# A decoder block with routed experts: another way through the router, and six weight chunks issued from ScalarE

## The reference, cut to what matters

```python
u = rmsnorm(h, norm_mix_w)
p = u @ w_in                       # pool | q,k,v | z | a | b | two branch gates
merged = sigmoid(gA) * pool_branch(p) + sigmoid(gB) * delta_net(p)   # 8 heads of 128
h = h + merged @ w_out
x = rmsnorm(h, norm_ffn_w)
group = argmax(softmax(x @ w_grp + b_grp))           # one of 4 groups
e1, e2 = top2(softmax((x @ w_rtr + b_rtr)[group]))   # two of the group's 8 experts
y = sum over e in (e1, e2) of weight_e * (silu(x @ w_gate[e]) * (x @ w_up[e])) @ w_down[e]
out = rmsnorm(h + y, norm_final_w)[meta:]
```

## Time and profile before

| | us |
|---|---|
| median of 3 runs | 868.41 |
| lowest, highest | 867.26, 871.16 |
| the profiled execution | 871.94 |
| its span | 870.2 |
| PE busy | 792.8 (91%) |
| DVE busy | 334.6 (38%) |
| ACT busy | 310.6 (36%) |
| moved by DMA | 239.96 MB, 276 GB/s on average |

### The profile page before, as it was taken

The page is one execution under the profiler, slowest core; times in us unless marked ns, Lnnn a source line. Parts: engine busy times, 40 slices in busy tenths (PEclk is TensorE's granted clock), DMA queues, the critical chain, the costliest instruction groups (busy, mean ns, idle before and its releaser), DMA issues.

```text
span 870.2 us, 14963 instructions
## 1 busy us (share of the span) xinstructions
PE 792.8 (91%) x5994; PEld 586.5 (67%) x5994; DVE 334.6 (38%) x795; ACT 310.6 (36%) x592; POOL 131.9 (15%) x147
## 2 busy tenths in 40 slices
PE   3789999999999999985999999999999888988884
PEld 2789999999999998545555655555555554555451
DVE  3462777776856665035212221122212211221113
ACT  4652856777567555131121221221211211112123
POOL 3181342442345026000000000000000000000000
PEclk9886999999999999985999999999999999999998
DMA  9323443333323514389899999999999999999991
GB/s 321 111 61 86 110 129 91 88 84 98 110 75 97 147 37 125 102 316 384 334 428 423 428 422 425 424 426 423 428 422 427 425 425 424 426 424 426 424 404 72
DMA packets 83661, 239.96 MB, mean 276 GB/s; under 512 B 7041, under 2 KB 65522, under 8 KB 67202
## 3 DMA queue, kind: packets, MB, share of 16 engines
q1 hardware_dynamic: 83122, 237.29, 70.0%
q10 hardware_dynamic: 464, 1.64, 0.5%
HBM read 237.87 MB, written 1.05 MB: 275 GB/s over the span
## 4 chain that ended last, share of the span: by engine, by line
PE 70%; DMA 19%; DVE 3%; ACT 3%; issue 2%; SPq 2%; POOL 0%; ACTq 0%; DVEq 0%; POOLq 0%
PE banks L1537 20%; DMA ring<-in_expert_w_up_dram 19%; PE banks L1790 17%; PE banks L1829 8%; PE banks L1710 3%; PE banks L1765 3%; PE banks L1801 2%; PE banks L1645 2%; PE banks L1647 2%; PE banks L1628 2%; SPq L655 1%; PE banks L1594 1%; PE banks L1700 1%; ACT bench L934 1%; PE banks L1532 1%
## 5 line engine op out<-in xcount | busy, mean ns | idle before, releaser
L1790 PE MATMUL banks<-ring,bench 128*64 128x256 f32 x2048 | 229.8, 380 | 17.7 <-DMA ring<-in_expert_w_up_dram 11.8
L1790 PEld LDWEIGHTS banks<-ring,bench 128*64 128x64 f32 x2048 | 148.8, 137 | 107.6 <-issue 25.0
L1537 PE MATMUL banks<-rounded 128*128 128x272 f32 (+2 forms) x1368 | 206.1, 300 | 2.9 <-DVE rounded L1145 2.8
L1537 PEld LDWEIGHTS banks<-rounded 128*128 128x128 f32 (+1 forms) x1368 | 180.8, 193 | 6.1 <-DVE rounded L1145 3.0
L1829 PE MATMUL banks<-ring,bench 128*64 128x512 f32 x512 | 116.9, 598 | 11.7 <-ACT bench L934 11.7
L1464 DVE TENSOR_TENSOR bench<-banks,bench 128x256 f32<-128x256 f32 x32 | 13.6, 425 | 244.8 <-PE banks L1790 185.8
L1829 PEld LDWEIGHTS banks<-ring,bench 128*64 128x64 f32 x512 | 33.9, 136 | 74.1 <-issue 54.8
L943 ACT ACTIVATE ysb<-banks 64x512 f32<-64x512 f32 x63 | 37.3, 592 | 119.4 <-PE banks L1829 118.6
L934 ACT ACTIVATE bench<-banks 128x256 f32<-128x256 f32 x32 | 12.3, 384 | 181.2 <-PE banks L1810 181.2
L741 ACT ACTIVATE rounded<-room 128x1024 fp32r<-128x1024 f32 x56 | 58.6, 1051 | 14.7 <-PE banks L1537 14.7
L1145 DVE TENSOR_TENSOR rounded<-room,rounded 128x1024 fp32r<-128x1024 f32 x42 | 55.5, 1323 | 17.4 <-ACT rounded L741 16.2
(11 more groups left out here) (265 smaller groups left out, 970.2 us busy)
## 6 DMA issues: line engine op xcount, KB each, us to landing
ring<-in_expert_w_gate_dram SPq DMA_DIRECT2D x32, 2048.0 KB, 30.6
ring<-in_expert_w_up_dram SPq DMA_DIRECT2D x32, 2048.0 KB, 32.1
ring<-in_expert_w_down_dram SPq DMA_DIRECT2D x64, 1024.0 KB, 29.2
room<-in_w_in_dram SPq DMA_DIRECT2D x56, 512.0 KB, 3.8
room<-in_w_out_dram SPq DMA_DIRECT2D x8, 512.0 KB, 3.5
hres<-in_x_dram ACTq DMA_DIRECT2D x2, 512.0 KB, 4.9
poolw<-in_pool_w_dram SPq DMA_DIRECT2D x4, 256.0 KB, 4.4
wfin<-in_norm_final_w_dram SPq DMA_DIRECT2D x1, 512.0 KB, 14.3
```

Source lines behind the costliest of these rows:

```text
L1537: ins = T.matmul(o, a, b[:, k, lo_at:L], start=(k == 0 and n == 0), stop=(k == KT - 1 and n == 2))
L1790: ins = T.matmul(pb[1 + c][half * 64:half * 64 + SLOTS, 0:256], xgT[:, q % ROOMS, kt, j * SLOTS:(j + 1) * SLOTS], w[:, kt, half * 256:(hal ...
```

## The change

- **Residual.** The first output step of each token tile starts its two banks with an identity matmul of `hres`. VectorE's adds and the four later identity matmuls are gone. The residual sum stays in banks 0 to 3, and all later uses of banks change places (routing and experts use 4 to 7).
- **Raw sums.** ScalarE and VectorE copy the banks of one token tile each to `xn`, in transposed order and not normalized. Transposes, gains and logits work on these sums; the reciprocal root is applied to the logits (with the bias in one operation) and in `xhi` and `xlo`. ScalarE evicts the transposed parts 6 and 7, VectorE the six others.
- **Router.** Expert columns come ahead of group columns. Many pairs of operations on two token tiles become one operation on both. `hot` is made with one comparison for each token tile. Six matmuls with no use for the result stand behind the logits.
- **First gather.** All four parts with `xhi`, then all four with `xlo`. The arithmetic of the weights, `most` and `xlo` are moved behind `hot`. The first gate matmuls start with two parts in place.
- **DMA.** `win` moves to the end of `room` (place 8 of the ring). Six chunks, (0, down) to (2, up), are issued by ScalarE once it has finished its part of the mixers. The router loads are issued by SP ahead of `w_out` block 3.
- The planner's cost of the first output steps is raised by 1.72 us.

```diff
+EARLY = [(0, 2), (1, 0), (1, 1), (1, 2), (2, 0), (2, 1)]
+BY_ACT = (6, 7)
...
-            op(("outk", k, i), "pe", 1.72, when(("mix", k), ("land", n), ("outk", k - 1, i) if k else None, ("outk", k, 0) if i else None),
+            op(("outk", k, i), "pe", 1.72 + (0 if k else 0.86 * 2), when(("mix", k), ("land", n), ("outk", k - 1, i) if k else None, ("outk", k, 0) if i else None),
...
-        win = take(WIN_SLOTS * D).rearrange("p (s k c) -> p s k c", s=WIN_SLOTS, k=KT)
+        win = room[:, room.shape[1] - WIN_SLOTS * D:].rearrange("p (s k c) -> p s k c", s=WIN_SLOTS, k=KT)
...
@@ SP
                 sp.dma_start(wout[:, n % WIN_SLOTS, :], w_out[0, k * P:(k + 1) * P, :]).then_inc(win_land[n % WIN_SLOTS], 16)
-
-            filled(sp, ("proj", len(TILES) - 1))
-            load_chunk(0, 2)
-            load_chunk(1, 0)
-            filled(sp, ("m", HEADS - 1, 1))
-            sp.dma_start(routw[:, :, 0:GROUPS], router_group_w[0].rearrange("(p k) n -> p k n", p=P)).then_inc(S("rout_land"), 16)
...
+                if k == WIN_SLOTS - 1:
+
+                    filled(sp, ("m", HEADS - 1, 1))
+                    sp.dma_start(routw[:, :, 0:EXPERTS], router_expert_w[0].rearrange("(p k) n -> p k n", p=P)).then_inc(S("rout_land"), 16)
...
-                        if again or (e and (e, c) != (1, 0)):
-                            load_chunk(e, c)
+                        if again or (e and (e, c) not in EARLY):
+                            load_chunk(sp, e, c)
@@ ScalarE
+            filled(act, ("proj", len(TILES) - 1))
+            filled(act, ("oT", HEADS - 1))
+            for e, c in EARLY:
+                load_chunk(act, e, c)
             warm(ACT.Sqrt, 2)
+            act.wait_ge(S("outproj"), 1)
+            for half in range(2):
+                nc.scalar.activation(turned(0)[:, 64 * half:64 * half + 64, :], pb[half].rearrange("p (q k) -> p q k", k=KT), ACT.Copy).then_inc(S("hp0"), 1)
...
+                nc.scalar.activation(junk2, xn[:, i, :], ACT.Square, scale=1.0 / 32.0, accum_out=rs[:, i, 0:1]).then_inc(S("ms"), 1)
...
+            for k in BY_ACT:
+                act.wait_ge(S("turned"), KT + k + 1)
+                nc.scalar.activation(x2T[:, k, :], pb[4 + k % 3][:, 0:SEQ], ACT.Copy, scale=gain[:, k:k + 1]).then_inc(S("uT"), 1)
+            act.wait_ge(S("rinv"), 1)
+            for i in range(TT):
+                nc.scalar.activation(xhi[:, i, :], xn[:, i, :], ACT.Copy, scale=rs[:, i, 1:2]).then_inc(S("xhi"), 1)
@@ VectorE
+            dve.wait_ge(S("outproj"), 1)
+            for half in range(2):
+                V.tensor_copy(turned(1)[:, 64 * half:64 * half + 64, :], pb[2 + half].rearrange("p (q k) -> p q k", k=KT)).then_inc(S("hp1"), 1)
...
+            both(lambda i: V.scalar_tensor_tensor(rt[:, i, 0:2, :].rearrange("p a c -> p (a c)")[:, 0:36], pb[7][:, 64 * i:64 * i + 36],
+                                                  rs[:, i, 1:2], rbias[:], ALU.mult, ALU.add))
...
+            V.scalar_tensor_tensor(plan[:, :, 0:TT].rearrange("p e t -> p t e"), pb[7][:, 128:192].rearrange("p (t e) -> p t e", t=TT), 1.0, row(8),
+                                   ALU.add, ALU.mult).then_inc(S("plan"), 1)
...
+            def settle():
+
+                weigh()
+                dve.wait_ge(S("total"), 1)
+                chain(V.max(most[:], pb[5][:, 192:224]))
+                V.tensor_copy(mosti[:], most[:, 0:1]).then_inc(S("most"), 1)
+                dve.wait_ge(S("xhi"), TT)
+                for i in range(TT):
+                    V.scalar_tensor_tensor(xlo[:, i, :], xn[:, i, :], rs[:, i, 1:2], xhi[:, i, :].bitcast(F32), ALU.mult, ALU.subtract).then_inc(S("xlo"), 1)
...
                 slots_of(0)
+                if not again:
+                    settle()
                 for part in range(PARTS):
                     bring(0, part)
+                if not again:
+                    weighed()
@@ TensorE
                         if k == 0:
                             bank(pe, ("out", 2 * i + half))
+                            pe.wait_ge(S(f"x_land{i}"), 16)
+                            T.matmul(pb[2 * i + half], ident[:], hres[:, i, half * 512:(half + 1) * 512], start=True, stop=False, skip_group_check=True)
...
-            for i in range(TT):
-                for half in range(2):
-                    pe.wait_ge(S("res"), 2 * i + half + 1)
-                    ins = T.matmul(pb[4 + 2 * i + half], ident[:], hres[:, i, half * 512:(half + 1) * 512], start=True, stop=True, skip_group_check=True)
...
+            for k in range(6):
+                T.matmul(pb[4][:, 0:SEQ], ident[:], x2T[:, k, :], start=True, stop=True)
             pe.wait_ge(S("picked"), 1)
+            T.matmul(pb[7][:, 128:160], before[:], rt[:, 0, 8, :], start=True, stop=True)
+            T.matmul(pb[7][:, 160:192], ones[:], rt[:, 0, 8, :], start=True, stop=False)
+            T.matmul(pb[7][:, 160:192], before[:], rt[:, 1, 8, :], start=False, stop=True).then_inc(S("pos"), 1)
+            T.matmul(pb[5][:, 192:224], ones[:], rt[:, 0, 8, :], start=True, stop=False)
+            T.matmul(pb[5][:, 192:224], ones[:], rt[:, 1, 8, :], start=False, stop=True).then_inc(S("total"), 1)
...
+                def gather_first():
+
+                    pe.wait_ge(S("hot"), 1)
+                    per = KT // PARTS
+                    for x, made in ((xhi, "xhi"), (xlo, "xlo")):
+                        pe.wait_ge(S(made), TT)
+                        for part in range(PARTS):
+                            if x is xhi and part == 1:
+                                pe.wait_ge(S("most"), 1)
...
+                            if first and c == 0:
+                                pe.wait_ge(S("xgT"), max(2, kt * PARTS // KT + 1))
```

More of the change, by code:

```diff
@@ L645, in _ @@
                 load_tile(n)
[L647 to L655, removed]
             for c in range(2):
-                load_chunk(0, c)
+                load_chunk(sp, 0, c)
             sp.dma_start(wfin[:], norm_final_w[None, :].to_broadcast([P, D])).then_inc(S("wf_land"), 16)
@@ L1378, in _, with row @@
[L1378 to L1382 removed]
+            def row(a, n=1):
+                return rt[:, :, a, :] if n == 1 else rt[:, :, a:a + n, :]
@@ L1730, in _ @@
                 ins.then_inc(S("turned"), 1)
             pe.wait_ge(S("rout_land"), 64)
-            for i in range(TT):
-                for k in range(KT):
-                    pe.wait_ge(S("uT" if k % 2 else "uTd"), k // 2 + 1)
-                    ins = T.matmul(pb[3][:, 64 * i:64 * i + 36], x2T[:, k, i * P:(i + 1) * P], routw[:, k, :], start=(k == 0), stop=(k == KT - 1))
-                ins.then_inc(S("logits"), 1)
-            pe.wait_ge(S("picked"), 1)
-            T.matmul(pb[3][:, 128:160], before[:], rt[:, 0, 8, :], start=True, stop=True).then_inc(S("pos"), 1)
@@ L1740, in _ @@
-            pe.wait_ge(S("picked"), 2)
-            T.matmul(pb[3][:, 160:192], ones[:], rt[:, 0, 8, :], start=True, stop=False)
-            T.matmul(pb[3][:, 160:192], before[:], rt[:, 1, 8, :], start=False, stop=True).then_inc(S("pos"), 1)
-            T.matmul(pb[3][:, 192:224], ones[:], rt[:, 0, 8, :], start=True, stop=False)
-            T.matmul(pb[3][:, 192:224], ones[:], rt[:, 1, 8, :], start=False, stop=True).then_inc(S("pos"), 1)
+            for k in range(KT):
+                cast_off(k)
+                for i in range(TT):
+                    ins = T.matmul(pb[7][:, 64 * i:64 * i + 36], x2T[:, k, i * P:(i + 1) * P], routw[:, k, :], start=(k == 0 and i == 0), stop=(k == KT - 1),
+                                   skip_group_check=True)
@@ L1777, in gate_up @@
                     first = e == 0 and not again
-                    pe.wait_ge(S("xgT"), parts + PARTS * (q + 1))
+                    if not first:
+                        pe.wait_ge(S("xgT"), parts + PARTS * (q + 1))
                     for c, name in ((0, "gate"), (1, "up")):
@@ L1828, in down @@
                         for half in range(2):
-                            ins = T.matmul(pb[3][half * 64:half * 64 + SLOTS, :], hT[:, b, side * 64:side * 64 + SLOTS],
+                            ins = T.matmul(pb[7][half * 64:half * 64 + SLOTS, :], hT[:, b, side * 64:side * 64 + SLOTS],
                                            w[:, side, b, half * 512:(half + 1) * 512], start=(f == 0), stop=(f == 3), skip_group_check=True)
                     ins.then_inc(S("y"), 1)
-                for part in range(PARTS):
-                    gather(0, part)
+                if again:
+                    for part in range(PARTS):
+                        gather(0, part)
+                else:
+                    gather_first()
                 for e in range(EXPERTS):
```

191 lines of the change are left out of this document (94 added, 97 removed).

## The result

The changed kernel takes 888.91 us, median of 4 runs (886.77 to 891.94), beside 869.78 us for the kernel before (4 runs, 867.26 to 871.63): a ratio of 1.0226, interval 1.0197 to 1.0255. It is 19 us slower, where 860.7 was forecast. The profiled execution took 891.94 us (span 890.1) against 871.94, so +20.0. Two later executions of the kernel before took 2,741 us, and no median or ratio here has them in it.

What follows compares the result with a forecast made beforehand. The expert weight stream was taken to bound the kernel, its end set by the first gate. Routing -15.1, residual matmuls +3.4 and late tile 3 +4.0 gave -7.7 us: 871.94 to 864.2, median 860.7; range 854 to 887.

Steps and rivals of the forecast that it cites:

- block 3 of w_out: Output weights on SP behind the router loads: tile 3 lands some 4 us late beside ScalarE's chunks, +4.0 us.
- rival 1: SP starves beside ScalarE's chunks, queues taking turns by packet: output projection ends at 409.0, +27.5 us, median 884.2; chance 0.36.
- some 0.5 us of issue: SP's four router loads ahead of tile 3: each takes some 0.5 us to issue, so tile 3 goes out at 361.4.
- Routing: From output projection to first gate: 38.4 us shrinks to 23.3, 15.1 less; bounds 21.1 and 27.1.
- Logits ready: After the output projection, copies, transposes, gains and logits: 8.0 us taken, between 6.2 and 9.5.
- Positions: Position matmuls behind six filler matmuls: 1.6 us, plus 0.2 for filler sticking out, bounds 0 and 2.2.
- Choosing: Small operations that choose experts: 4.4 us falls to 3.0, thirteen steps becoming twelve, seven of them one operation for two.
- plan and masks: After the positions: 4.7 us becomes 1.0, with one operation and two wide comparisons.
- gather and gate: Last part of routing, up to the first gate's end: 9.8 us becomes 9.3 to 9.8, 9.5 taken.
- the residual matmuls: Four identity matmuls in the output projection, on a TensorE busy throughout: eight rows at 0.43 us, +3.4 us.
- the first gate sets the end: Expert weight stream: moving the first gate by one us moves the end by one, if nine chunks are there.
- Rival 3: Chunks land after the gate, so DMA or ring takes over: gain only 5.8 us, 862.6; held by the forecast's chance, 0.54.

Runs made afterwards that it cites:

- run 6: The changed kernel with ScalarE's six chunks issued as 16 DMAs with rows of 1 KB; 874.21 us, ratio 1.0042.
- run 5: The changed kernel with router weights loaded contiguous in each partition and repacked by VectorE, 32 small packets per engine in place of 144; 884.3 us, ratio 1.0167.
- after: The changed kernel as made, against the kernel before; 888.91 us, ratio 1.0226.
- run 2: The changed kernel with ScalarE waiting for the last w_out block before it sends its six chunks; 865.25 us, ratio 0.9937 to the kernel before.
- run 11: The changed kernel with ScalarE's chunks sent after the last w_out block and the six filler matmuls left out; 866.44 us, ratio 0.9956.
- run 9: The changed kernel with ScalarE's chunks sent after the last w_out block landed and router loads behind that block; 865.19 us, ratio 0.9958.
- run 7: The changed kernel with ScalarE's chunks sent after the last w_out block and six more filler matmuls behind the output projection; 864.95 us, ratio 0.9938.
- run 8: The changed kernel with 1 KB rows in ScalarE's chunks, router loads behind the last w_out block and six more filler matmuls; 880.18 us, ratio 1.0114.
- run 3: The changed kernel with the whole fetch of the kernel before, all chunks and router loads on SP; 866.46 us, ratio 0.9961.

## Why the prediction was wrong

**The step that failed** is the one for block 3 of w_out: "If SP gets half of the bandwidth, tile 3 lands some 4 us late". SP got half of the packets, and of the bytes 1 to 2% (0.02 of 2.07 MB, 0.04 of 2.19). The working of rival 1 held nearly to the digit: block 3 was to land at 391.8 and landed at 390.07; the output projection was to end at 409.0 and ended at 409.04. Without the wait it would have ended at 382.1 (364.85, when the 16 rows behind 357.94 are done, plus 40 of 0.432), so the term was +26.9 us where +4.0 stood. Of this 25.4 is the wait, and 1.5 is that the 40 rows behind it took 18.84 us instead of 17.3, with 0.69 granted in 390 to 395. That rival 1 met the end of the output projection to 0.04 us is luck in the last digits: the block came 1.7 us earlier than it said, and the rows behind it took 1.7 us longer.

**Why I chose so.** Two rows spoke of two queues at work. The earlier trace rows gave 121 to 118 packets at ten times the bytes, and the earlier trace rows 1,293 to 29. I let the second weaken the first. But a count tells of turns only where both queues have something waiting, and in the earlier trace rows ScalarE's queue was busy for 12.3% of the time: it may have been empty, as I wrote myself. The equal count could hardly come about by chance; the unequal one had a plain other reason. The Trainium skill (DMA: Bandwidth & Descriptors, Queues, rings and completion order) says that an engine serves its queues in turn and changes at packet boundaries. The trace agrees, with 154 to 155, 278 to 277 and 143 to 144 here, and 1,404 to 1,406 in run 6. The same section of the Trainium skill gives 9 to 17 descriptors as typical of such a packet; here a turn was one row, as the stretches of 0.62 us show, and the measurement decides.

A second reading was wrong. For each router load I took "some 0.5 us of issue", from the 0.66 of the group load. The next lines of the same timeline of the kernel before say otherwise:

```profile
370.35 8.60 SPq L675 DMA_DIRECT2D poolw<-in_router_expert_w_dram  x1
378.99 3.45 SPq L676 DMA_DIRECT2D rbias<-in_router_group_b_dram  x1
```

No rival had a held issue in it. It is not the main cause: in run 5, without it, block 3 still landed at 384.6 (390.07 in after).

**The term that was mis-sized.** Routing was to shrink from 38.4 to 23.3 us and shrank to 28.9, beyond my bound of 27.1. Without a long stand of TensorE ahead of it, it took 26.0 us in run 2, 24.7 in run 11 and 29.2 in run 9, so whether the stand made it longer stays open. The chain of after from the output projection on:

```profile
409.06 2.43 ACT late L901 x2
...
412.69 2.30 PE banks L1757 x10
414.99 6.67 PE banks L1763 x32
421.67 5.27 PE banks L1768 x12
...
429.58 2.40 DVE xlo L1429 x2
```

- Logits ready 12.6 us after the output projection's end; 8.0 taken, 9.5 as the bound. The copies take 2.4 us (1.30 to 1.36 us for each bank), not 1.4. They also turn the layout, but that is not all of it: in runs 9 and 11, where ScalarE began 1.3 and 0.3 us behind VectorE and not together with it, the same copies took 1.01 to 1.03 us each. Why they take longer when both engines begin at once is not shown. All transposes go ahead of the logits, where I had let the logits run beside the gain copies. And the logits took 6.67 us, at the lower level of the clock: 0.50 granted in 415 to 420. In run 2, at 1.00 for the first two thirds of them, they took 4.07, and were ready 9.7 us after.
- Positions: six filler matmuls took 5.27 us at the lower level and ended 1.7 us behind the choice of experts (425.23). That is within my bounds of 0 and 2.2, but near the upper one, where I took 0.2. Run 11, without them, has a stretch shorter by 1.3 us.
- Choosing took 3.45 us (3.0 taken), the position matmuls 0.9 (1.6), plan and masks 1.1 (1.0), gather and gate 9.0 (9.5). These held within half a us, but for the positions, which took 0.7 less.

**The part of the sum that held:** the residual matmuls, eight rows of 0.43 us, cost 3.4 us on a TensorE without gaps. And the first gate sets the end as long as DMA waits for it: gate +21.4 us, last landing +20.8, span +19.9.

**The sum again.** Rival 1 said -15.1 + 3.4 + 27.5 = +15.8. With what was measured, -9.5 + 3.4 + 26.9 is +20.8; another 0.6 is that this execution came later to its last output rows, together the gate's +21.4. The span grew by 19.9. The range ended at 887, at rival 1 with 3 us over, so it left the routing's upper bound out on exactly that side; 888.9 is beyond it.

**Rival 3** was not tried by the change as made, but it is what run 2 became: with a late stream nothing starves, the stream's start takes over as the bound, and the time is 865, not the 860.7 of the forecast. Runs 2, 7 and 9 gain 5.2, 5.8 and 4.6 us. No run has an early stream and block 3 in time together, so whether the forecast's 7.7 us were to be had is not shown. An estimate from these runs: 382.1 and run 2's 26.0 us put the gate at 408.1, 8.4 us before the 416.54 of before. The best that was found, 864.95 to 865.25 us (runs 2, 7 and 9), is 0.4 to 0.6% under the kernel before; the three can't be told apart.

## What to carry to other kernels

Before a load is moved to a second queue, count packets, not bytes: in these runs, while both queues had work, each packet of the one cost the other one packet's time (0.51 us beside rows of 8 and 16 KB), so a matrix of 128-byte rows waited for the whole stream. Send the small and the awaited loads first, and let the heavy stream wait for their landing; here one wait was worth 24 us. And ask of every engine that feeds a queue what it can't do while its issue is held.

## What the runs showed that I had not expected

- The issue of a DMA can hold its engine long. SP stood 22.96 us in one issue of 16 KB with the two router weight loads ahead of it; ScalarE up to 8.82 us in run 8. A second queue is not needed for it: in run 3, with everything on SP, L681 took 7.93 us. With 16 small packets for each engine ahead (run 5) no issue took over 0.44, and with the loads of after but no stream beside them (run 2) 0.71. Which count of waiting packets makes an issue stand was not tried.
- The clock fell to its lower level in run 7 although TensorE was busy for 19.0 of 20 us, with 0.58 granted in 390 to 395.
- With rows of 1 KB in place of 8 and 16 KB, and w_out's rows of 4 KB beside them, the engines moved 360 GB/s in place of about 425 (run 6, 375 to 400 us).
